# Fewer calls for the expert dot products inside the top-k heads, more of them in the later stages

## The chip, the cores and the metric

The kernel runs on one core of one Trainium2 chip. The metric is the device time of one execution in microseconds; lower is better. In the profile, PE is TensorE, DVE is VectorE, ACT is ScalarE, POOL is GpSimd and SP is SyncE.

## The reference

Two layers on 512 tokens of width 1024. Each layer is a mixer (attention with a convolution in layer 0, gated linear attention in layer 1) and a PEER block, which retrieves single-neuron experts. The change touches the PEER block alone; RMS norms and the mixers are left out here:

```python
def block(xb):                                   # 128 tokens
    q = (xb @ w_query).reshape(t, PEER_HEADS, 2, PEER_HALF)          # 8 heads
    scores = jnp.einsum('thpd,hpnd->thpn', q, sk)                    # 2 x 128 keys
    s_val, s_idx = lax.top_k(scores, PEER_TOPK)                      # 16
    cand = s_val[:, :, 0, :, None] + s_val[:, :, 1, None, :]
    c_val, c_idx = lax.top_k(cand.reshape(t, PEER_HEADS, 256), PEER_TOPK)
    ...
    expert = i1 * N_KEYS + i2                                        # of 16384
    gate = jax.nn.softmax(c_val, axis=-1)
    act = jax.nn.gelu(jnp.einsum('thkd,td->thk', expert_u[expert], xb))
    return jnp.einsum('thk,thkd->td', gate * act, expert_v[expert])
```

Each token has 8 heads times 16 picks, 128 experts.

## The kernel before, in words

The 512 tokens are split into four tiles of 128. **Three of them (384 tokens) take the dense way**: TensorE computes the activations of all 16384 experts and the sum over all of them, with gates that are zero where an expert is not picked. **The first tile takes the gathered way**: for each of its 128 picks GpSimd fetches one row of `u` per token, and later one row of `v` per token, by an indirect DMA (L452), 128 rows of 4 KB (524,288 bytes) at once, into a ring of five buffers (`NBUF`). VectorE consumes them. `dots` (L965, its instruction is L969) multiplies a fetched row by the normalised input and sums it up to one column of `hg`; `sums` (L974, its instruction is L978) adds a fetched row of `v`, times its coefficient, to the residual `x[:, 0]`. Each frees its buffer for the next fetch (`gat_free`). A layer has 128 dots and then 128 sums. Between them ScalarE applies the gelu to `hg` and VectorE multiplies by the gates.

Every matrix of experts is read in float32 and split into two bf16 halves: ScalarE writes the high half (`split_hi`, L630) and VectorE the low half (`split_lo`, L941, called as `ahead(n)` for tile n). TensorE waits for both before each tile (L1479 to L1481, 24 matmuls) and before each quarter of a value group (L1547).

The PEER block of a layer goes through these stages, in the same order on all engines:

- **Heads**, h = 0 to 7. TensorE does eight tiles per head; behind the first it computes the queries of the head (L1490, evicted by ScalarE at L665), behind the second the scores (L1497, L671). VectorE does the top-k of the head for all four token tiles (L991 to L1057), a chain of small instructions with drains between them. It ends with the index of the experts of the first token tile (`eidx`, L1062), which releases 16 more fetches. Between the steps of the chain stand `ahead(RING * h + 4)` to `ahead(RING * h + 11)` and, by hand, calls of `dots`. In head h only rows of earlier heads are there to be taken, so head 0 has none.
- **Tail of the heads**, tiles 64 to 71. TensorE transposes the picks (L1509), ScalarE exponentiates (L708), VectorE makes the gates (L1072 to L1076), TensorE transposes them (L1514).
- **Batches**, tiles 72 to 119. For each tile VectorE builds one-hot matrices (L1096 to L1100), TensorE multiplies them (L1526, L1527), and so a dense matrix of gates for the 384 tokens is made. It goes to DRAM, as do the activations. Tiles 120 to 127 follow without batches.
- **Values**, groups k = 0 to 31 of 72 matmuls each. For each group SyncE loads 2 MB of `v`, the activations (768 KB) and the gates (640 KB). VectorE multiplies them (`scale(k)`, L1111 to L1116), ScalarE rounds the product (`high(k)`, L693), VectorE makes the rest (`low(k)`, L1120), and TensorE waits for that before the group (`clo_ready`). VectorE then does the four low halves of group k + 1.

The last dot must come before the gelu of `hg`, which stands in group `HG_GROUP`; sums begin there. The last sum must come before the residual of token tile 0 is closed, after group 31.

Of the kernel before, what the change touches and what calls it, by code (L numbers as in the profile page):

```python
# [15 lines left out]
P = 128  # L16
# [17 lines left out]
PH = 8  # L34
# [14 lines left out]
NBUF = 5  # L49
NST = NCK - 2  # L50
B0 = NK // 2 + 8
HG_GROUP = 3
CAND = 128


# [30 lines left out]
def build(nc, x_d, cols_d, const_d, hot_d, relb_d, wmix_d, wz_d, wg2_d, wq_d, u_d, ur0_d, ur1_d, v0_d, v1_d,  # L86
# [7 lines left out]
    with ExitStack() as ctx:  # L94
# [369 lines left out]
        def _(act):  # L464
# [167 lines left out]
            def peer(L):  # L632
                T0, G0 = STREAM * L, 2 * NG * L
                def ahead(n):
                    if n < TPG:
                        act.wait_ge(first_in[n], 16 * (L + 1))
                    split_hi(T0 + n, n % RING, arrival(L, n) if n >= TPG and n % TPG == 0 else None)
# [74 lines left out]
                for k in range(NG):  # L712
                    if k:
                        high(k)
                    if k + 1 < NG:
                        for q in range(TPG):
                            ahead(NK + TPG * (k + 1) + q)
                    if k == HG_GROUP:
                        act.wait_ge(hg_ready, L + 1)
# [11 lines left out]
        def _(dve):  # L731
# [211 lines left out]
            def peer(L):  # L943
                T0, G0 = STREAM * L, 2 * NG * L
                def ahead(n):
                    if n < TPG:
                        dve.wait_ge(first_in[n], 16 * (L + 1))
                    split_lo(T0 + n, n % RING, arrival(L, n) if n >= TPG and n % TPG == 0 else None)
# [8 lines left out]
                taken = [0]  # L957

                def taken_in():
                    n = 2 * P * L + taken[0]  # L960
                    taken[0] += 1
                    dve.wait_ge(gat_in[n % NBUF], 16 * (n // NBUF + 1))
                    return ring[n % NBUF], (n % P)

                def dots(count):  # L965
                    for _ in range(count):
                        if taken[0] < P:
                            row, g = taken_in()
                            dve.tensor_tensor_reduce(row, row, xg, 1.0, 0.0, ALU.mult, ALU.add,  # L969
                                                     hg[:, g:g + 1]).then_inc(gat_free, 1)  # L970
                            if taken[0] == P:
                                dve.drain().then_inc(hg_ready, 1)

                def sums(count):  # L974
                    for _ in range(count):
                        if taken[0] < 2 * P:
                            row, g = taken_in()
                            dve.scalar_tensor_tensor(x[:, 0], row, cf[:, g:g + 1], x[:, 0], ALU.mult, ALU.add).then_inc(gat_free, 1)  # L978
                            dve.drain()

                for h in range(PH):
# [1 line left out]
                    ahead(RING * h + 4)  # L983
                    ahead(RING * h + 5)

                    late = 0 < h < PH - 1
                    dots(3 if h else 0)
                    dve.wait_ge(s_out, h + (PH * L + 1))
                    ahead(RING * h + 6)
                    for tt, s in pairs:  # L990
# [2 lines left out]
                    for tt, s in pairs:  # L993
                        dve.max_index(idx[:, tt, s, 0:8].bitcast(U32), val[:, tt, s, 0:8], sc[:, tt, s])
                        dve.match_replace(sc2[:, tt, s], val[:, tt, s, 0:8], sc[:, tt, s], -3e38)
                    dots(1 if h else 0)
                    dve.drain()
                    for tt, s in pairs:
                        dve.max(val[:, tt, s, 8:16], sc2[:, tt, s])
# [1 line left out]
                    ahead(RING * h + 7)  # L1001
                    for tt, s in pairs:
                        dve.max_index(idx[:, tt, s, 8:16].bitcast(U32), val[:, tt, s, 8:16], sc2[:, tt, s])
                    dots(2 if h else 0)
                    dve.memset(cand[:, :, 64:80], -3e38)
                    for first, rows, width in ((0, 4, TOPK), (4, TOPK - 4, 4)):
                        a = val[:, :, 0, first:first + rows].unsqueeze(3).to_broadcast([P, TT, rows, width])
# [5 lines left out]
                    for tt in range(TT):  # L1013
                        dve.max(cval[:, tt, 0:8], cand[:, tt])
                    ahead(RING * h + 8)
                    dots(1 if h else 0)
                    dve.drain()
                    for tt in range(TT):
                        dve.max_index(cidx[:, tt, 0:8].bitcast(U32), cval[:, tt, 0:8], cand[:, tt])
# [2 lines left out]
                    for tt in range(TT):  # L1022
                        dve.max(cval[:, tt, 8:16], cand2[:, tt])
                    ahead(RING * h + 9)
                    dots(1 if h else 0)
                    dve.drain()
                    for tt in range(TT):
                        dve.max_index(cidx[:, tt, 8:16].bitcast(U32), cval[:, tt, 8:16], cand2[:, tt])
# [10 lines left out]
                    dve.tensor_tensor(side, ci, shift, ALU.logical_shift_right)  # L1039
                    dve.tensor_tensor(rank[1].bitcast(U32), ci, low, ALU.bitwise_and)  # L1040
                    ahead(RING * h + 10)
                    dots(1 if late else 0)
                    dve.drain()
                    dve.tensor_scalar(rank[0].bitcast(U32), side, TOPK - 1, None, ALU.bitwise_and)
                    dve.drain()
                    for s in range(2):
# [7 lines left out]
                        if s == 0:  # L1054
# [6 lines left out]
                    at = slice(h * TOPK, (h + 1) * TOPK)  # L1061
                    dve.scalar_tensor_tensor(eidx[:, at], picks[:, 0, 0, at], float(NK), picks[:, 1, 0, at],  # L1062
                                             ALU.mult, ALU.add).then_inc(eidx_ready, 1)
                    dots(3 if late else 0)

                dve.drain()
                pv = picks[:, 2].rearrange("p a (h k) -> p (a h) k", h=PH)
# [24 lines left out]
                def hots(b):  # L1092
                    hot = [oh[:, k, b % 2].rearrange("p (a n c) -> p a n c", n=P, c=2) for k in range(3)]
                    every = iota_2[:].unsqueeze(1).to_broadcast([P, BT // 2, P, 2])
                    dve.wait_ge(g_built, NB * L + b + 1)
                    dve.tensor_tensor(hot[1], every, along(1, b), ALU.is_equal)  # L1096
                    dve.tensor_tensor(hot[0], every, along(0, b), ALU.is_equal)
                    dve.drain()
                    dve.tensor_tensor(hot[2], hot[1], along(3, b), ALU.mult)
                    dve.tensor_tensor(hot[1], hot[1], along(2, b), ALU.mult).then_inc(oh_ready, 1)  # L1100

                def scale(k):


                    s, g = k % 2, (k + NG - 2) % NG
                    if k < 2:
                        dve.wait_ge(gelu_done, NK * L + TPG * (g + 1) + 2)
                    dve.wait_ge(gh_in[s], (32 * (NG // 2) - 16) * L + 16 + 32 * (k // 2))
                    h4 = hst[s].rearrange("p q (c t) -> p q c t", t=CHK)
                    early = h4[:, :, 0:NST]  # L1110
                    dve.tensor_tensor(early, early, gr[s].rearrange("p c q t -> p q c t"), ALU.mult)  # L1111
                    dve.wait_ge(g_read, NB * (L + 1) + 2)
                    for c in range(2):
                        late = h4[:, :, NST + c]
                        dve.tensor_tensor(late, late, gst[c][:, g].rearrange("p (q t) -> p q t", q=TPG), ALU.mult)
                    dve.drain().then_inc(cf_ready, 1)  # L1116

                def low(k):
                    dve.wait_ge(chi_ready, NG * L + k + 1)
                    dve.tensor_tensor(clo[k % 2], hst[k % 2], chi[k % 2], ALU.subtract).then_inc(clo_ready, 1)  # L1120

                for n in range(NK // 2 + 3, NK):
                    if B0 <= n < B0 + NB:
                        hots(n - B0)
                    ahead(n + TPG)
                    if n == NK - 4:
                        scale(0)
                    if n == NK - 2:
                        low(0)
                    if B0 <= n < B0 + NB:  # L1130
                        dots(n % 2)
                    elif B0 <= n < NK - 2:
                        dots(2)
                for q in range(TPG):
# [4 lines left out]
                for k in range(NG):  # L1139
                    if k > 1:  # L1140
                        scale(k)
                        if k > HG_GROUP:
                            sums(1)
                        else:
                            dots(1)
                        low(k)
                    if 0 < k < NG - 1:
                        for q in range(TPG):
                            ahead(NK + TPG * (k + 1) + q)
                    if k < HG_GROUP:  # L1150
                        dots(4 if k else 2)
                    else:
                        if k == HG_GROUP:
                            assert taken[0] == P
                            dve.wait_ge(hg_act, L + 1)
                            dve.tensor_tensor(cf, hg, gt[:, 0], ALU.mult)
                            dve.drain()
                        sums(4)
                assert taken[0] == 2 * P
                dve.drain().then_inc(x_new, 1)  # L1160
                for tt in range(GT, TT):
# [22 lines left out]

            mixer0()
            peer(0)
            mixer1()
            peer(1)


# [470 lines left out]
```

## Time and profile before

| | |
|---|---|
| time, median of 3 runs | 2967.38 us (2964.68 to 2969.16) |
| the profiled execution | 2967.38 us, its span 2965.6 us |
| TensorE busy | 2882.7 us, 97% of the span |
| VectorE busy | 2318.7 us, 78% |
| ScalarE busy | 1010.6 us, 34% |
| GpSimd busy | 731.3 us, 25% |
| chain that ended last | TensorE 68%, VectorE 19% |
| DMA | 775.21 MB, mean 261 GB/s |

The difference of 1.8 us between an execution and its span lies outside the instructions. In layer 0 the head stage runs from about 276 to 662 us, its tail to 700, the batches to 932, and the value stage from 966 to 1460. Layer 1 has the same stages from about 1772 us on.

### The profile page before, as it was taken

To read this page: it belongs to the slowest core of one execution; us is meant where nothing else is said; L and a number is where in the kernel's file an instruction comes from. 1 tells how busy PE (TensorE), PEld (TensorE's weight loads), DVE (VectorE), ACT (ScalarE), POOL (GpSimd) and SP (SyncE) were. 2 spreads that over 40 slices of the span, in tenths; PEclk is the share of its full clock that TensorE was granted. 3 is DMA by queue.
4 is the path that set the end of the run, shared out by engine and by line. 5 is a ranking of instruction groups with operands and counts; after the bars stand their busy time and mean duration, and the time that the engine had idled before them with its cause. 6 is when DMAs were issued, how large, how long until landed. Compare 5 with 4: busy or idle time off the path is not lost.

```text
span 2965.6 us, 39736 instructions
## 1 busy us (share of the span) xinstructions
PE 2882.7 (97%) x14563; PEld 1527.8 (52%) x14632; DVE 2318.7 (78%) x4251; ACT 1010.6 (34%) x1335; POOL 731.3 (25%) x518
## 2 busy tenths in 40 slices
PE   8998999999999999999999889999999999999998
PEld 4454555556666444444444445555556664444443
DVE  5853799998888899999400336999988888999995
ACT  2162323224554333333321122232245544333333
POOL 0000133330112445544000001232301124445540
PEclk9999999999999999999999999999999999999999
DMA  4202577776998999999211124777769989999993
GB/s 151 85 29 108 212 261 291 259 263 223 320 310 311 388 404 394 397 395 390 73 63 70 57 94 181 260 283 257 259 237 308 308 317 399 391 396 400 394 400 116
DMA packets 210407, 775.21 MB, mean 261 GB/s; under 512 B 15445, under 2 KB 97497, under 8 KB 190218
## 3 DMA queue, kind: packets, MB, share of 16 engines
q1 hardware_dynamic: 45698, 416.58, 36.9%
q0 software_dynamic: 73728, 268.47, 24.4%
q10 hardware_dynamic: 90888, 89.14, 8.6%
q8 instruction: 32, 0.52, 0.1%
q14 instruction: 61, 0.50, 0.0%
HBM read 681.59 MB, written 92.54 MB: 261 GB/s over the span
## 4 chain that ended last, share of the span: by engine, by line
PE 68%; DVE 19%; issue 4%; DMA 3%; DVEq 3%; PEld 1%; ACT 1%; PEldq 0%; ACTq 0%; POOL 0%; SPq 0%
PE ps L1547 28%; PE ps L1479 6%; PE ps L1481 6%; PE ps L1480 6%; PE ps L1231 5%; PE ps L1240 5%; DVE arena L969 5%; PE ps L1260 3%; DVE arena L941 3%; DMA arena<-in_ur,arena 3%; PE ps L1490 2%; PE ps L1527 1%; PE ps L1526 1%; PEld ps L1547 1%; DVE arena L1053 1%
## 5 line engine op out<-in xcount | busy, mean ns | idle before, releaser
L1547 PE MATMUL ps<-arena 128*128 128x512 bf16 x4541 | 992.2, 379 | 5.3 <-DVE arena L1120 1.5
L452 POOL DMA_INDIRECT arena<-in_ur,arena x256 | 331.2, 1294 | 1679.8 <-DVE arena L969 948.3
L1547 PEld LDWEIGHTS ps<-arena 128*128 128x128 bf16 x4608 | 450.5, 98 | 546.4 <-issue 2.9
L941 DVE TENSOR_TENSOR arena<-arena 128x1024 bf16<-128x1024 f32 x512 | 611.5, 1220 | 130.4 <-ACT arena L630 88.4
L1479 PE MATMUL ps<-xnh,arena 128*128 128x384 bf16 x2048 | 673.1, 329 | 32.6 <-DVE xnl L767 13.3
L1481 PE MATMUL ps<-xnh,arena 128*128 128x384 bf16 x2048 | 673.4, 329 | 0.0
L1480 PE MATMUL ps<-xnl,arena 128*128 128x384 bf16 x2048 | 673.2, 329 | 0.0
L630 ACT ACTIVATE arena<-arena 128x1024 bf16<-128x1024 f32 x512 | 525.5, 1049 | 186.8 <-PE ps L1547 104.3
L452 POOL DMA_INDIRECT arena<-in_v,arena x256 | 399.1, 1559 | 406.2 <-DVE x_res L978 339.5
L978 DVE SCALAR_TENSOR_TENSOR x_res<-arena,x_res 128x1024 f32<-128x1024 f32 x256 | 328.6, 1283 | 20.8 <-issue 0.4
L969 DVE CUSTOM_DVE_ANT_0 arena<-arena 128x1024 f32<-128x1024 f32 x256 | 306.3, 1219 | 34.2 <-DMA arena<-in_ur,arena 33.5
L657 ACT ACTIVATE arena<-ps 128x384 f32<-128x384 f32 x256 | 125.6, 491 | 531.7 <-PE ps L1481 520.4
L1479 PEld LDWEIGHTS ps<-xnh,arena 128*128 128x128 bf16 x2048 | 201.5, 98 | 168.6 <-issue 45.7
L1481 PEld LDWEIGHTS ps<-xnh,arena 128*128 128x128 bf16 x2048 | 201.6, 98 | 135.7 <-issue 4.8
L1480 PEld LDWEIGHTS ps<-xnl,arena 128*128 128x128 bf16 x2048 | 201.6, 98 | 131.5 <-issue 10.3
L693 ACT ACTIVATE arena<-arena 128x1536 bf16<-128x1536 f32 x64 | 94.9, 1483 | 507.6 <-DVEq L1116 507.6
L1490 PE MATMUL ps<-xnT,arena 128*128 128x512 f32 x512 | 222.3, 592 | 0.0
L1490 PEld LDWEIGHTS ps<-xnT,arena 128*128 128x128 f32 x512 | 96.8, 190 | 115.8 <-issue 114.8
L1231 PE MATMUL ps<-xnT,arena 128*128 128x512 f32 (+1 forms) x336 | 148.5, 605 | 2.5 <-ACT xnT L487 2.5
L1240 PE MATMUL ps<-arena,xnT 128*128 128x512 f32 x320 | 139.1, 598 | 0.0
L1120 DVE TENSOR_TENSOR arena<-arena 128x1536 bf16<-128x1536 f32 x64 | 112.5, 1758 | 21.8 <-ACT arena L693 21.8
L504 ACT ACTIVATE arena<-ps 128x512 f32<-128x512 f32 (+1 forms) x49 | 29.1, 597 | 266.3 <-PE ps L1231 130.3
(188 smaller groups left out, 2322.9 us busy)
## 6 DMA issues: line engine op xcount, KB each, us to landing
arena<-in_v SPq DMA_DIRECT2D x64, 2048.0 KB
arena<-in_u SPq DMA_DIRECT2D x62, 2048.0 KB
h_scratch<-arena ACTq DMA_DIRECT2D x60, 768.0 KB
arena<-h_scratch SPq DMA_DIRECT2D x60, 768.0 KB
arena<-gate_scratch SPq DMA_DIRECT2D x64, 640.0 KB
arena<-in_wmix SPq DMA_DIRECT2D x15, 2048.0 KB, 7.9
gate_scratch<-xnT ACTq DMA_DIRECT2D x10, 2048.0 KB
gate_scratch<-arena ACTq DMA_DIRECT2D x10, 2048.0 KB
```

The source lines that it names most:

```text
L452: pool.indirect_dma_start(ring[n % NBUF], None, ur_d[L] if g < P else vr_d[L], at).then_inc(gat_in[n % NBUF], 16)
L630: act.activation(hi[:, s], raw[s // TPG][:, s % TPG], ACT.Copy).then_inc(hi_ready, 1)
L941: dve.tensor_tensor(lo[:, s], raw[s // TPG][:, s % TPG], hi[:, s], ALU.subtract).then_inc(lo_ready, 1)
L969: dve.tensor_tensor_reduce(row, row, xg, 1.0, 0.0, ALU.mult, ALU.add, hg[:, g:g + 1]).then_inc(gat_free, 1)
L978: dve.scalar_tensor_tensor(x[:, 0], row, cf[:, g:g + 1], x[:, 0], ALU.mult, ALU.add).then_inc(gat_free, 1)
L1231: last = pe.matmul(bank[0:cols_of], wblk[b % 2][:, kd, at], xnT[:, kd], start=kd == 0, stop=kd == KD - 1)
L1240: last = pe.matmul(bank, xnT[:, kd, at], wblk[b % 2][:, kd], start=kd == 0, stop=kd == KD - 1)
L1479: pe.matmul(ps[:, j % 2, 0:TD], uh, xnh[:, kd], start=kd == 0, stop=False)
L1480: pe.matmul(ps[:, j % 2, 0:TD], uh, xnl[:, kd], start=False, stop=False)
L1481: last = pe.matmul(ps[:, j % 2, 0:TD], ul, xnh[:, kd], start=False, stop=kd == KD - 1)
L1490: last = pe.matmul(ps[:, 2 + s], wq[:, kd, at], xnT[:, kd], start=kd == 0, stop=kd == KD - 1)
L1547: last = pe.matmul(ps[:, 2 + 2 * tt + dh], c, v[:, TPG * s + q, dh * 512:(dh + 1) * 512], start=False, stop=stop and c is cl)
```

## The change

Two numbers for the calls of `dots` replace hand-placed ones. In a head, the calls between the steps of the top-k chain go; four rows are taken before the wait for the scores, and in heads 1 to 6 five more behind the index. In the batch stage two of three tiles have a dot instead of every second. In the value stage group 0 has four dots at its end instead of two, and the gelu of `hg`, with the first sums, moves from group 3 to group 6.

```diff
+HEAD_DOTS = 9
+V_DOTS = 5
-HG_GROUP = 3
+HG_GROUP = 6
...
-                    late = 0 < h < PH - 1
-                    dots(3 if h else 0)
+                    if h:
+                        dots(HEAD_DOTS // 2)
                     dve.wait_ge(s_out, h + (PH * L + 1))
...
-                    dots(1 if h else 0)
...
-                    dots(2 if h else 0)
+
...
-                    dots(1 if h else 0)
...
-                    dots(1 if h else 0)
...
-                    dots(1 if late else 0)
...
                     dve.scalar_tensor_tensor(eidx[:, at], picks[:, 0, 0, at], float(NK), picks[:, 1, 0, at],
                                              ALU.mult, ALU.add).then_inc(eidx_ready, 1)
-                    dots(3 if late else 0)
+                    if 0 < h < PH - 1:
+                        dots(HEAD_DOTS - HEAD_DOTS // 2)
...
                     if B0 <= n < B0 + NB:
-                        dots(n % 2)
+                        dots(1 if n % 3 else 0)
                     elif B0 <= n < NK - 2:
                         dots(2)
...
                     if k < HG_GROUP:
-                        dots(4 if k else 2)
+                        dots(V_DOTS - 1)
                     else:
                         if k == HG_GROUP:
-                            assert taken[0] == P
                             dve.wait_ge(hg_act, L + 1)
                             dve.tensor_tensor(cf, hg, gt[:, 0], ALU.mult)
                             dve.drain()
-                        sums(4)
+                        sums(V_DOTS - 1)
```

A call of `dots` takes no row once all 128 are taken.

## Rows read from the trace of the kernel before

**Rows 1.** Busy time in stages: batches, start of values, the rest (layer 0)

```profile
core 0: us, PE busy (x) PEld busy (x) DVE busy (x) ACT busy (x) POOL busy (x), PEclk, DMA share, GB/s
...
700.00:932.00 232.00, 232.00 (x1920) 156.84 (x1919) 205.16 (x288) 119.44 (x144) 26.35 (x23) 1.00 0.88 298
...
966.00:998.00 32.00, 31.13 (x143) 14.03 (x146) 26.86 (x34) 12.93 (x13) 13.93 (x9) 1.00 0.98 402
998.00:1405.00 407.00, 405.63 (x1860) 184.54 (x1887) 382.93 (x347) 140.42 (x132) 196.58 (x128) 1.00 1.00 396
```

**Rows 2.** Waits of TensorE, heads and tail, layer 0, then layer 1

```profile
PE ps L1479 <- issue: 9.7, 6, 3.0
...
PE ps L1479 <- DVE arena L941: 6.4, 3, 3.0
PE ps L1479 <- issue: 3.2, 3, 1.4
PE ps L1509 <- DVE arena L1057: 0.9, 1, 0.9
```

**Rows 3.** Timelines of VectorE and TensorE (start, duration, what, [idle before])

```profile
513.87 1.21 DVE L941 TENSOR_TENSOR arena<-arena 128x1024 bf16<-128x1024 f32 x1
...
515.17 0.32 PE L1479 MATMUL ps<-xnh,arena 128*128 128x384 bf16 x1 [2.99 <-issue]
```

**Rows 4.** Busy time in the first and last of six stretches

```profile
516.30:519.70 3.40, 3.40 (x13) 1.65 (x11) 3.32 (x21) 1.06 (x1) 0.94 (x1) 0.50 0.96 357
...
2178.60:2182.00 3.40, 3.00 (x10) 1.46 (x11) 1.95 (x5) 2.50 (x3) 0.00 (x0) 0.50 0.01 5
```

**Rows 5.** Query evictions, heads 0 to 4; indices, heads 1 to 3; index, head 0

```profile
L665 ACT ACTIVATE arena<-ps x5: 1024/1024/1025, 296.2 to 483.0; 128x1024 f32<-128x1024 f32 x5
...
L1062 DVE SCALAR_TENSOR_TENSOR arena<-arena x3: 175/175/176, 388.5 to 484.8; 128x16 uint32<-128x16 f32 x3
...
335.24 0.18 DVE L1062 SCALAR_TENSOR_TENSOR arena<-arena 128x16 uint32<-128x16 f32 x1
```

**Rows 6.** Timelines of VectorE and TensorE, start of the values, layer 0

```profile
976.47 1.22 DVE L969 CUSTOM_DVE_ANT_0 arena<-arena 128x1024 f32<-128x1024 f32 x1
...
977.62 1.22 DVE L969 CUSTOM_DVE_ANT_0 arena<-arena 128x1024 f32<-128x1024 f32 x1
...
994.75 1.22 DVE L969 CUSTOM_DVE_ANT_0 arena<-arena 128x1024 f32<-128x1024 f32 x1 [2.76 <-DMA arena<-in_ur,arena]
...
998.00 5.34 PE L1547 MATMUL ps<-arena 128*128 128x512 bf16 x24 [0.77 <-DVE arena L1120]
```

**Rows 7.** Timeline of GpSimd in head 6; list of DMA issues

```profile
636.09 1.68 POOL L452 DMA_INDIRECT arena<-in_ur,arena  x1 [9.53 <-DVE arena L969]
...
642.63 0.94 POOL L452 DMA_INDIRECT arena<-in_ur,arena  x1 [0.30 <-issue]
...
arena<-in_u SPq DMA_DIRECT2D x8, 512.0 KB, 5.5
```

**Rows 8.** Timelines of the three engines in the tail, layer 0

```profile
681.82 0.87 PE L1509 MATMUL ps<-const,arena 128*128 128x128 f32 x6 [0.93 <-DVE arena L1057]
...
684.59 0.63 ACT L708 ACTIVATE arena<-arena 128x512 f32<-128x512 f32 x1
...
687.04 2.35 DVE L941 TENSOR_TENSOR arena<-arena 128x1024 bf16<-128x1024 f32 x2
```

**Rows 9.** Groups of instructions of the value stage (busy, mean ns, idle before)

```profile
L978 DVE SCALAR_TENSOR_TENSOR x_res<-arena,x_res 128x1024 f32<-128x1024 f32 x256 | 328.6, 1283 | 20.8 <-issue 0.4
...
L1120 DVE TENSOR_TENSOR arena<-arena 128x1536 bf16<-128x1536 f32 x64 | 112.5, 1758 | 21.8 <-ACT arena L693 21.8
L1111 DVE TENSOR_TENSOR arena<-arena 128x1280 f32<-128x1280 f32 x64 | 95.4, 1491 | 5.4 <-issue 0.4
L693 ACT ACTIVATE arena<-arena 128x1536 bf16<-128x1536 f32 x64 | 94.9, 1483 | 507.6 <-DVEq L1116 507.6
```

**Rows 10.** Timeline of VectorE, start of the values, layer 1

```profile
2487.20 1.23 DVE L969 CUSTOM_DVE_ANT_0 arena<-arena 128x1024 f32<-128x1024 f32 x1 [1.73 <-DMA arena<-in_ur,arena]
```

**Rows 11.** Timeline of VectorE, end of the values, layer 0

```profile
1454.05 1.22 DVE L1164 TENSOR_TENSOR x_res<-x_res,ps 128x1024 f32<-128x1024 f32 x1 [13.28 <-PEq L1571]
```

## The prediction

> **What bounds the kernel now.** I read the busy time by stage first. TensorE works without a break in the batch stage (232.0 of 232 us) and for 405.6 of 407 us of the value stage, and VectorE is never its equal there, 205.2 and 382.9 us [rows 1]. So the kernel is bound by TensorE, and another engine costs time only where TensorE stands. The list of waits gives those places [rows 2]: in the head stage and the four tiles behind it, layer 0 has six waits of 9.7 us in all and one of 0.9 us before the transposes of the picks; layer 1 has 6.4, 3.2 and again 0.9 us. Together that is 21.1 us. Some of these waits carry no releaser, but the two timelines side by side name it: VectorE ends the low half of tile 40 (`ahead(RING * h + 8)` of head 4) at 513.87 + 1.21 = 515.08, and TensorE, idle for 2.99 us, starts that tile at 515.17 [rows 3]. Layer 1 names L941 outright.
>
> Each larger stall also costs clock. Six stretches of 3.4 us, each beginning a microsecond or so after the engine resumed work, or at it, ran with a granted clock of 0.50, the 1.2 GHz level; the first and the last stand in [rows 4]. At half speed 3.4 us do 1.7 us of work, so the six lose 10.2 us. In all 21.1 + 10.2 = 31.3 us hang on VectorE being late in the head stages. That is the most that lighter heads can give back.
>
> **Why VectorE is late.** TensorE's own period per head is (483.0 - 296.2) / 4 = 46.7 us, by the evictions of the queries; VectorE's, from index to index over heads 1 to 3, is (484.8 - 388.5) / 2 = 48.15 us [rows 5]. It falls 1.45 us behind per head, uses up its lead by head 4, and from then on TensorE pays: stalls before heads 5 and 7, and at the end of the stage, where tiles follow each other without the queries between them.
>
> **The change part by part.** Two dots in a row are 1.15 us apart (976.47 and 977.62) [rows 6]. Counting calls:
>
> - Heads 1 to 6 hold 3+1+2+1+1+1+3 = 12 dots each now, head 7 holds 8. They will hold 4+5 = 9, and 4. Per layer 80 become 58.
> - Batch stage: 24 become 32. The six tiles behind it keep 12, and one stays at the start of the value stage. So 103 instead of 117 are taken when group 0 begins.
> - Value stage: group 0 has 4 instead of 2, groups 1 and 2 have the same 4 and 5, and the dots then run on into group 5. Sums start in group 6 instead of 3 and end in group 31 instead of 28, five per group as before.
>
> *Heads.* 3 x 1.15 = 3.4 us less makes VectorE's period 48.15 - 3.4 = 44.7 us, 2.0 us under TensorE's. Head 0 has no dots, and its index comes at 335.24, 7.7 us before the next eviction of queries (296.2 + 46.7 = 342.9) [rows 5], that is some 10 us after the first tile of the next head began. From the scores on, a head will run as head 0 does, so this place repeats. The critical low half (`+ 8`) stands the same steps ahead of the index as now, less three dots, and so comes several microseconds before its tile (I reckon 6). The stalls before heads 5 and 7 go: 2.99 + 0.33 + 3.00 us and two slow stretches in layer 0, 6.4 us and two in layer 1, so 19.5 us.
>
> *The burst.* Five dots behind the index, two low halves and four dots make nine rows nearly in a row, with five buffers. Four rows must be fetched meanwhile. GpSimd needs 0.94 us for a fetch when VectorE is elsewhere and 1.68 when it runs dots [rows 7], so with the gaps between them issues lie some 2 us apart, the fourth at about 8 us. A 512 KB load lands 5.5 us after its issue where DMA is not crowded [rows 7], so the ninth row comes some 13 us after the burst began; the dots are done at 14 to 14.5 us instead of 12.7 (five dots, two low halves, four dots). VectorE has 2.0 us to spare there, because it would otherwise wait for the scores. I cost this at nothing. With 3 us of waiting per burst the period would be 47.7 and the lead used up again by the last head (a rival below).
>
> *End of the heads.* The index of head 7 comes some 10 us earlier, so the waits before tiles 65 and 66, the transposes and tile 68 go: 4.3 and 4.1 us, and one slow stretch each. What is late next is the gate chain. The transposes end at 681.82 + 0.87 = 682.69, the exponential behind a table load at 684.59 + 0.63, the gates at about 687.1, and the low half of tile 69 1.15 us later, 688.2 [rows 8]: 5.5 us after the transposes. TensorE will fill that with one tile at full clock and three transposes, 4.4 us. It keeps about 1.3 us per layer with the wake-ups. The tails give 6.05 - 1.3 and 5.8 - 1.3, together 9.2 us.
>
> So the head side gives 19.5 + 9.2 = 28.7 us.
>
> *Batch stage.* Eight more dots are 9.2 us, and VectorE stood 26.8 of 232 us there [rows 1]. Two tiles with a dot and one without average less than a tile of TensorE, and a row has more than a tile's time to arrive. Cost: nothing; bound: the 9.2 us if that cover were gone.
>
> *Start of the value stage.* Here DMA moves 402 GB/s with its engines 98% busy [rows 1], and refills are late already. In layer 0 the row that goes into the buffer of the dot of 977.62 (five rows on) is the one that VectorE waits for until 994.75, 17 us later. `low(2)` hangs on it, and TensorE waits 0.77 us for `low(2)` at 998.00 [rows 6]. With two more dots in group 0 the two rows that group 1 now takes from full buffers are gone, so that late row becomes the third of group 1's four instead of the single one behind `scale(2)`. The two next rows, 524 KB each at 402 GB/s, land 1.3 us apart, at 996.0 and 997.3. The working: fourth dot until 997.2; `scale(2)` 1.49 and twice 0.28 with its drain, 2.0 us, 999.2; ScalarE's `high(2)` 1.48, 1000.9; `low(2)` 1.76, 1002.6 [rows 9]. TensorE starts group 2 at 1002.8 instead of 998.0: 4.9 us. In layer 1 the same row comes at 2487.20, so that `low(2)` ended 1.16 + 1.76 later, at 2490.1 [rows 9, 10]; by the steps above it will end at 2495.0, and of the 4.9 us I take 1.0 as margin, since TensorE did not wait there: 3.9 us. Waits of 3 us cost a slow stretch [rows 3, 4], so 1.7 us each on top. Sum: 8.8 + 3.4 = 12.2 us. Lower bound 0 (the refills come when wanted); upper bound some 9 us more per layer, if each extra refill comes as late after its forerunner as this one did. I take the middle, worked from the rows of this very place.
>
> A rule speaks against this cost. The Trainium skill (DMA: Bandwidth & Descriptors, "Anatomy of one DMA — SWDGE (gpsimd) path") puts a DMA issued from GpSimd at 2.0 us plus bytes over 436 GB/s. By that estimate a row takes 3.2 us, no refill would be late and the time would be that of the first rival. The 17 us in the trace do not agree.
>
> *The rest of the value stage.* Per group the load stays. At its end three sums (1.28 us each [rows 9]) come behind `low(31)`, where VectorE now stands 13.28 us [rows 11]. Nothing.
>
> **The sum.** 28.7 - 12.2 = 16.5 us less. The profiled execution took 2967.38 us with a span of 2965.6, and is itself the median of the three runs: 2967.4 - 16.5 = 2950.9, say 2951 (-0.56%).
>
> **The rivals.**
>
> 1. The refills are not late at the value stage's start, for instance because the next 2 MB load also starts later. Then 2967.4 - 28.7 = 2939. Against it stands DMA at 98%. Chance 0.18.
> 2. The burst of nine starves. At 3 us lost per burst the period is 47.7, 1.0 over TensorE's; the lead lasts through the heads, but the tail's 9.2 us are not won: 2967.4 - 19.5 + 12.2 = 2960. At 3.4 us the period is today's, 48.15, nothing of the 28.7 is sure, and the kernel is slower by up to the 12.2. For it: fetches that take nearly twice as long beside dots [rows 7]. Against it: DMA is not crowded at that place, and half the burst finds its rows in the buffers. Chance 0.15. In the Trainium skill (Trainium Architecture — The Big Picture, "What this means for kernel authors") the port pair of VectorE and GpSimd is an exclusive lock rather than a split of bandwidth. Were GpSimd shut out for the whole burst, this rival would be the outcome; a fetch of 1.68 us during dots shows a delay and not a stop.
> 3. Slower: the debt is never repaid. Five rows and the loads of v, h and gates are about 6.2 MB per group of 15.4 us, 400 GB/s, and DMA already gives 396 at a share of 1.00 [rows 1]. If two early rows push the h and gate loads late in every later group, `scale(k)` and TensorE with it slip each time. It decides from 28.7 / 58 = 0.5 us per group; at 1 us the time is 2967 - 29 + 58 = 2996. Against it: the same rate runs today with TensorE idle for 1.4 of 407 us, and a wait of 5 us at group 2 lets DMA move 2 MB. Chance 0.08.
>
> **How the numbers follow.** My forecast has 0.52, with a range of its own of 2945 to 2956; 0.07 stays for what I don't see. The range of 2938 to 2964 takes in rival 1 and the milder end of rival 2, and leaves out the third. A measurement here tells 0.2%, 6 us, from no change: faster is my case, rival 1 and half of rival 2, 0.78; same is a third of rival 2 and most of the unseen, 0.12; slower is rival 3 and the worst of rival 2, 0.10.
>
> **What would show it.** After: no TensorE wait of 3 us in the head stage and no slow clock there; VectorE's idle time there now waits for ScalarE's scores; index to index 46.7 us from head 1 on; about 1.3 us of idle between the gate transposes and tile 69. At group 2 of each layer a wait of 4 to 6 us for `low` (L1120 now), behind dots that wait for DMA. Wrong would be: waits of that kind in every group, waits for fetched rows of over 3 us in each head, or none at group 2.

## The result and the profile after

| | before | after |
|---|---|---|
| median, side by side on one chip | 2968.27 us (2964.68 to 2969.21) | 2992.11 us (2980.25 to 2996.37) |
| the profiled execution, its span | 2967.38 us, 2965.6 us | 2995.14 us, 2993.3 us |

The change makes the kernel slower by 0.7%: ratio 1.0073, 95% interval 1.0045 to 1.0100. The forecast was 2951.0, its range ended at 2964. The spread has grown too: 16 us between executions instead of 5 (8 us in the 19 executions of the kernel before that stand beside the last experiments).

I cut both traces at the evictions of the dense tiles (L657 before, L659 now: tiles 0, 63, 71, 119, 127) and at the first and last matmul of the values. The differences are those of the two profiled executions.

| stage | layer 0, before to after | layer 1 | change | forecast |
|---|---|---|---|---|
| heads | 378.9 to 380.3 | 378.8 to 377.4 | 0.0 | -19.5 |
| tail | 38.9 to 37.1 | 38.6 to 35.8 | -4.6 | -9.2 |
| batches | 230.3 to 238.4 | 230.4 to 238.9 | +16.6 | 0 |
| values | 499.8 to 506.8 | 497.9 to 507.0 | +16.1 | +12.2 |
| all else | | | -0.3 | 0 |
| span | | | +27.8 | -16.5 |

Busy time by stage in the kernel after, layer 0, answers to [rows 1] (columns as there):

```profile
core 0: us, PE busy (x) PEld busy (x) DVE busy (x) ACT busy (x) POOL busy (x), PEclk, DMA share, GB/s
288.00:662.00 374.00, 366.17 (x1879) 208.28 (x1877) 313.37 (x1037) 106.12 (x140) 92.09 (x63) 0.99 0.62 223
...
700.00:940.00 240.00, 233.25 (x1926) 156.05 (x1924) 210.84 (x302) 118.78 (x145) 36.51 (x32) 1.00 0.89 304
972.00:1012.00 40.00, 34.61 (x150) 15.13 (x151) 32.35 (x41) 13.02 (x13) 18.03 (x10) 0.92 0.96 385
1012.00:1425.00 413.00, 411.58 (x1887) 187.15 (x1912) 381.18 (x359) 141.30 (x132) 201.80 (x130) 1.00 0.99 391
```

The batch stage, where TensorE had not stood at all, now has 6.75 us in which it does. TensorE's waits in heads and tail, then in the batches, of each layer (us in total, times, longest) answer to [rows 2]:

```profile
PE ps L1477 <- issue: 8.3, 6, 3.0
PE ps L1477 <- ACT arena L632: 1.6, 1, 1.6
PE ps L1507 <- DVE arena L1055: 0.7, 1, 0.7
...
PE ps L1477 <- DVE arena L943: 5.4, 2, 2.7
PE ps L1477 <- issue: 1.8, 2, 1.4
...
PE ps L1524 <- DVE arena L1099: 6.7, 6, 1.9
...
PE ps L1524 <- DVE arena L1099: 7.4, 6, 2.1
```

The stalls in the heads have moved and not gone, and six waits per layer for the one-hots (L1099) have come. The third new place is group 2 of the values. VectorE and TensorE there, layer 0, then the same wait in layer 1; this answers to [rows 6]:

```profile
990.34 1.22 DVE L971 CUSTOM_DVE_ANT_0 arena<-arena 128x1024 f32<-128x1024 f32 x1
992.82 1.23 DVE L971 CUSTOM_DVE_ANT_0 arena<-arena 128x1024 f32<-128x1024 f32 x1 [1.25 <-DMA arena<-in_ur,arena]
995.42 1.23 DVE L971 CUSTOM_DVE_ANT_0 arena<-arena 128x1024 f32<-128x1024 f32 x1 [1.37 <-DMA arena<-in_ur,arena]
1000.99 1.22 DVE L971 CUSTOM_DVE_ANT_0 arena<-arena 128x1024 f32<-128x1024 f32 x1 [4.33 <-DMA arena<-in_ur,arena]
...
1005.61 1.76 DVE L1119 TENSOR_TENSOR arena<-arena 128x1536 bf16<-128x1536 f32 x1 [0.19 <-ACT arena L695]
...
1007.61 2.72 PE L1545 MATMUL ps<-arena 128*128 128x512 bf16 x6 [5.29 <-ACT arena L632]
...
2516.88 3.57 PE L1545 MATMUL ps<-arena 128*128 128x512 bf16 x8 [6.69 <-ACT arena L632]
```

The releaser printed is not the last one: `low(2)` ends at 1005.61 + 1.76 = 1007.37, and TensorE starts at 1007.61.

### The profile page after: what moved, and what is told of

The parts are those of the page before. It is cut to its first block, busy times and chain, and to the rows that moved or that the text cites. A ratio compares the mean times of both kernels' runs of the same rounds, so it can differ in the third digit from the quotient of the medians.

```text
span 2993.3 us, 39736 instructions
## 1 busy us (share of the span) xinstructions
PE 2889.2 (97%) x14563; PEld 1528.3 (51%) x14632; DVE 2320.4 (78%) x4251; ACT 1008.0 (34%) x1335; POOL 763.3 (25%) x518
## 4 chain that ended last, share of the span: by engine, by line
PE 49%; DVE 16%; issue 12%; PEld 8%; DMA 5%; DVEq 4%; ACT 2%; POOL 2%; ACTq 1%; PEldq 1%; SPq 0%
PE ps L1545 13%; PEld ps L1545 8%; PE ps L1477 5%; PE ps L1478 5%; PE ps L1479 5%; PE ps L1229 5%; PE ps L1238 5%; DMA arena<-in_ur,arena 4%; DVE arena L943 4%; PE ps L1258 3%; POOL arena L454 2%; PE ps L1488 2%; PE ps L1524 1%; PE ps L1525 1%; DVE arena L1051 1%
## 5 line engine op out<-in xcount | busy, mean ns | idle before, releaser
L454 POOL DMA_INDIRECT arena<-in_ur,arena x256 | 364.4, 1423 | 1758.7 <-DVE arena L971 1004.1
L1545 PEld LDWEIGHTS ps<-arena 128*128 128x128 bf16 x4608 | 451.6, 98 | 560.4 <-ACT arena L632 12.9
L632 ACT ACTIVATE arena<-arena 128x1024 bf16<-128x1024 f32 x512 | 525.0, 1048 | 192.3 <-PE ps L1545 107.4
L659 ACT ACTIVATE arena<-ps 128x384 f32<-128x384 f32 x256 | 125.4, 490 | 532.6 <-PE ps L1479 532.4
```

The lines of the kernel that those rows point to most:

```text
L454: pool.indirect_dma_start(ring[n % NBUF], None, ur_d[L] if g < P else vr_d[L], at).then_inc(gat_in[n % NBUF], 16)
L632: act.activation(hi[:, s], raw[s // TPG][:, s % TPG], ACT.Copy).then_inc(hi_ready, 1)
L1545: last = pe.matmul(ps[:, 2 + 2 * tt + dh], c, v[:, TPG * s + q, dh * 512:(dh + 1) * 512], start=False, stop=stop and c is cl)
```

## The two mechanisms that I had not seen

**Batches.** A stretch of the three engines in the kernel after (start, duration, what, [idle before]): ScalarE issues the gate store, 8.6 us later the store of the activations (`h_store`, L663), and everything behind that issue shifts:

```profile
739.02 0.39 ACTq L687 DMA_DIRECT2D gate_scratch<-arena  x1
...
747.60 2.96 ACTq L663 DMA_DIRECT2D h_scratch<-arena  x1
...
750.60 1.06 ACT L632 ACTIVATE arena<-arena 128x1024 bf16<-128x1024 f32 x1 [1.99 <-issue]
...
751.69 1.23 DVE L943 TENSOR_TENSOR arena<-arena 128x1024 bf16<-128x1024 f32 x1 [2.38 <-ACT arena L632]
...
752.84 1.22 DVE L971 CUSTOM_DVE_ANT_0 arena<-arena 128x1024 f32<-128x1024 f32 x1
...
756.69 0.23 PE L1524 MATMUL ps<-arena 128*128 128x128 bf16 x1 [0.41 <-DVE arena L1099]
```

The issue holds ScalarE for 2.96 us, its high half (L632) comes late, VectorE's low half behind it, then the dot, then the one-hots. Nine of the twelve stores of this stage in layer 0 are issued like that, in 2.96 to 4.39 us. VectorE was busy for 210.84 us there and waited 24.2 us for the high half:

```profile
DVE arena L943 <- ACT arena L632: 24.2, 17, 3.1
```

That is 235.0 of 240 us. Cut at tiles 71 and 119, nothing is left over: 210.6 us busy, 24.2 in this wait and 3.6 in gaps of at most 0.15 us make the 238.4 of the stage. So VectorE's chain was the bound. In the kernel before, the same wait in 700 to 932 us had already been

```profile
DVE arena L941 <- ACT arena L630: 25.4, 35, 2.7
```

and with 205.16 us of work that left 1.4 of 232 us free [rows 1], where I had counted 26.8 as room. The eight dots came on top of a wait that did not shrink to make room for them.

**Heads.** The burst behind the index of head 5, layer 0. Its nine dots are those of 580.08 to 584.66 (five) and of 588.08, 589.95, 597.14 and 598.42:

```profile
579.99 0.17 DVE L1060 SCALAR_TENSOR_TENSOR arena<-arena 128x16 uint32<-128x16 f32 x1
...
581.57 1.68 POOL L454 DMA_INDIRECT arena<-in_ur,arena  x1 [31.42 <-DVE arena L971]
...
583.56 1.99 POOL L454 DMA_INDIRECT arena<-in_ur,arena  x1 [0.30 <-issue]
...
585.59 0.34 ACTq L663 DMA_DIRECT2D h_scratch<-arena  x1
...
585.85 1.99 POOL L454 DMA_INDIRECT arena<-in_ur,arena  x1 [0.30 <-issue]
...
587.50 0.33 SPq L375 DMA_DIRECT2D arena<-in_wq  x1
...
589.95 1.23 DVE L971 CUSTOM_DVE_ANT_0 arena<-arena 128x1024 f32<-128x1024 f32 x1 [0.65 <-DMA arena<-in_ur,arena]
597.14 1.23 DVE L971 CUSTOM_DVE_ANT_0 arena<-arena 128x1024 f32<-128x1024 f32 x1 [5.96 <-DMA arena<-in_ur,arena]
...
608.49 1.23 DVE L943 TENSOR_TENSOR arena<-arena 128x1024 bf16<-128x1024 f32 x1
...
609.82 0.48 PE L1477 MATMUL ps<-xnh,arena 128*128 128x384 bf16 x1 [2.99 <-issue]
```

The second refill is there 6.4 us after its issue (583.56 to 589.95), the third only after 11.3 (585.85 to 597.14): the store of the activations (768 KB) was issued just before it, the next head's query weights (1152 KB) just behind it. The burst waits for 6.6 us where 2.0 were to spare, and from 606.83 TensorE stands for 2.99 us, for the low half that ends at 608.49 + 1.23. The store is issued 17.6 us after the eviction of tile 8h + 8 in heads 1 to 6, whatever VectorE does. The index comes 5.7, 6.7, 9.3 and 12.8 us after that eviction in heads 1 to 4. So each late burst puts more of the next one's refills behind the store: the lateness feeds itself, which fits the spread of the times. From index to index over heads 1 to 3 it is (476.9 - 379.8) / 2 = 48.5 us, where I had reckoned 44.7. Over the whole stage a fetch of a row takes 7.3 us in the median from issue to landing (4.9 to 11.5).

## The experiments

Medians; each ratio is to the kernel before on the same chip. The layers' stage lengths are cut as above.

**The batch pattern alone**, in the kernel before:

```diff
-                        dots(n % 2)
+                        dots(1 if n % 3 else 0)
```

> The kernel before with the batch stage alone changed (a dot in two of three tiles). Theory A (the batch stage's growth comes from where the dots stand: ScalarE is blocked for 3 to 4 us every fourth tile by its store of activations, and a dot in the tile behind that makes the one-hots late): TensorE waits for L1100 in about six tiles of each layer, batch stage 238 us instead of 230 in each, and with the earlier end of the dots about 2967 + 16 - 1 = 2982 us. Rival A' (it comes from the changed head stage or from fetches, not from this pattern): batch stage 230 us, time 2967.

2981.24 against 2963.93 us, ratio 1.0055 (1.0038 to 1.0072). Batches 240.1 and 238.4 us. TensorE's waits there, layer 0:

```profile
PE ps L1526 <- DVE arena L1100: 8.3, 6, 2.0
```

The eight dots cost about 17 us by themselves. As expected.

**Two more dots in value group 0 alone**, in the kernel before (groups 1 and 2 had four already):

```diff
-                        dots(4 if k else 2)
+                        dots(4)
```

> The kernel before with value group 0 alone changed (four dots for two). Theory B (refills late behind the two extra dots): TensorE waits 5 to 7 us before group 2 of each layer, followed by some 7 us at half clock, 3.4 us lost: 2967 + 18 = 2985 us. Rival B' (that wait is due to what happened earlier, since 103 and not 117 dots were taken by then): no wait above 1 us, 2967.

2982.14 against 2963.93 us, 1.0064 (1.0047 to 1.0081). The wait before group 2 is there without the rest of the change, 7.30 us in layer 0 and 7.56 in layer 1; the values take 508.8 and 508.0 us:

```profile
1000.44 4.00 PE L1547 MATMUL ps<-arena 128*128 128x512 bf16 x9 [7.30 <-ACT arena L630]
```

**Where the dots of the batches stand**, in the kernel after; 36 dots instead of 32, none where `n % 4` is 2:

```diff
-                        dots(1 if n % 3 else 0)
+                        dots(1 if n % 4 != 2 else 0)
```

> The changed kernel with a dot in every tile of the batch stage but those with n mod 4 = 2 (36 instead of 32 dots). Theory A (position): batch stage back to about 230 us in each layer although it has more dots, 2992 - 16 = 2976. Rival A'' (number: VectorE has too little time for more than 24): batch stage 238 us or more, 2992 or above.

2986.52 against 2963.93 us, 1.0087 (1.0066 to 1.0109). Batches 239.0 and 239.1 us:

```profile
PE ps L1524 <- DVE arena L1099: 6.2, 9, 1.0
```

Nine short waits in place of six longer ones, and nearly the same sum. My theory that the position alone was at fault fell: the stage did not come back to 230 us. The rival holds for the stage, though not for the time (2992 or above), and number alone does not carry it either: eight dots more cost 8 us, and these four, otherwise placed, only 0.2 to 0.6 more. How place and number share the loss stays open.

**Group 0 back to two dots**, in the kernel after:

```diff
-                        dots(V_DOTS - 1)
+                        dots(V_DOTS - 1 if k else 2)
```

> The changed kernel with two dots in value group 0 instead of four. Theory B: the waits of 5.3 and 6.7 us before group 2 shrink to about 1 us and the half clock behind them goes: 2992 - 17 = 2975. Rival B': the waits stay, 2992.

2971.61 against 2963.93 us, 1.0024 (1.0010 to 1.0039). No wait at group 2; the values take 498.9 and 498.0 us. Heads were 368.5 us in layer 0 and 382.8 in layer 1 of one execution: the instability in one trace.

**The same 58 dots per layer, but between the steps of the heads**, in the kernel after (the last added line stands at three places):

```diff
-                    if h:
-                        dots(HEAD_DOTS // 2)
+                    late = 0 < h < PH - 1
+                    dots(3 if h else 0)
...
+                    dots(1 if h else 0)
...
+                    dots(2 if late else 0)
...
+                    dots(1 if late else 0)
...
-                    if 0 < h < PH - 1:
-                        dots(HEAD_DOTS - HEAD_DOTS // 2)
```

> The changed kernel with the same 58 dots of the heads put back between the steps of the top-k chain (3+1+2+1+1+1 in heads 1 to 6, 3+1 in head 7). Theory C (the burst of nine starves on its refills once it meets the load of the next head's weights, and so the gain of lighter heads is lost): no TensorE wait of 3 us and no half clock in either head stage, heads 368 us per layer instead of 380 and 377, 2992 - 20 = 2972 us. Rival C' (VectorE's lateness there has another cause than the burst): stalls stay, 2992.

2971.39 against 2966.35 us, 1.0016 (1.0006 to 1.0025). Heads 368.5 us in both layers, with no wait of TensorE, and the store of the activations where it was: fewer dots do give the gain, the burst takes it back. VectorE waits for fetched rows for 4.8 us in each head stage (34.7 and 32.0 in the kernel after), and the index keeps its place, 12.5 to 12.9 us behind the tile in heads 1 to 6.

**The store of the activations two tiles earlier**, in the kernel after. It is then issued ahead of the gate store and not 8.6 us behind it:

```diff
+                    if n % TPG == TPG - 1 and n // TPG < NG - 2:
+                        h_store(n // TPG)
                     if B0 <= n < B0 + NB:
                         gates_out(n - B0)
-                    if n >= TPG and n % TPG == 1 and n // TPG - 1 < NG - 2:
-                        h_store(n // TPG - 1)
```

> The changed kernel with ScalarE's store of activations issued two tiles earlier, ahead of the store of gates instead of 9 us behind it. Theory A2 (the store stands in a queue still full of the gate store's packets and blocks ScalarE for 3 to 4 us, and the wait for the high half behind it takes the time that the eight extra dots need): L663 takes 0.3 us everywhere, no wait for L1099, batch stage 230 us instead of 238, 2992 - 16 = 2976. Rival A3 (VectorE's own work per tile is too long with 32 dots, whatever ScalarE does): L663 short, waits stay, 2992.

2951.91 against 2966.35 us, 0.9954 (0.9937 to 0.9971). Durations of the store's issue (minimum, median, maximum in ns) in the batches of layer 0, first in the kernel after, then here:

```profile
L663 ACTq DMA_DIRECT2D h_scratch<-arena x12: 338/3292/4392, 709.1 to 929.2; - x12
```

```profile
L663 ACTq DMA_DIRECT2D h_scratch<-arena x12: 338/338/352, 704.8 to 916.8; - x12
```

Batches are 230.3 us again with all 32 dots, and VectorE's wait for the high half, cut at tiles 71 and 119, falls from 24.2 to 15.2 us. That was expected; that the heads fell to 368.5 us as well, with TensorE busy throughout, was not:

```profile
283.00:666.00 383.00, 383.00 (x1983) 219.03 (x1983) 332.43 (x1085) 114.48 (x151) 91.97 (x63) 1.00 0.64 230
```

In head 5 of layer 0 the third refill is issued at 576.15 and the fourth at 578.44. Their dots wait little:

```profile
581.95 1.25 DVE L971 CUSTOM_DVE_ANT_0 arena<-arena 128x1024 f32<-128x1024 f32 x1 [1.20 <-DMA arena<-in_ur,arena]
...
584.72 1.22 DVE L971 CUSTOM_DVE_ANT_0 arena<-arena 128x1024 f32<-128x1024 f32 x1 [1.51 <-DMA arena<-in_ur,arena]
```

The third row takes 5.8 us instead of 11.3. These rows do not part two effects, since this burst also starts 3.8 us earlier behind its tile. And the burst is not cured: VectorE still waits 20.0 us for rows in the first head stage, and the index slips from 5.7 to 10.0 us behind the tile between heads 1 and 7. The stage ends before the lead is used up.

**The same earlier store in the kernel before.**

> The kernel before with the same earlier store. TensorE has no wait in its batch stage, so by theory A2 the time stays within 2 us of 2964; only L661 falls from 1.9 to 3.6 us to 0.3. By rival A3 the same, so this run tells only whether the earlier store costs anything by itself.

2950.84 against 2966.35 us, 0.9948 (0.9931 to 0.9964): a miss. Heads 371.7 us in both layers, batches unchanged at 230.3. TensorE's waits between tiles 0 and 63 of layer 0 were 6.3 us with two of 3.0, followed by two stretches at half clock. They are now 2.7 us, the longest 1.2, and no slow clock follows. The rows go on to 668 us and so take in some of the tail:

```profile
PE ps L1479 <- issue: 4.5, 5, 1.2
PE ps L1479 <- ACT arena L630: 1.4, 1, 1.4
```

VectorE's waits for fetched rows fall from 10.3 to 4.5 us. The kernel before paid for the same collision at its three trailing dots, and I had put all of it down to VectorE's work. That work is still too long by itself: the indices of heads 1 to 3 stand where they stood, 48.1 us apart, and 3.2 of the 10.4 us stay.

**Which place the store hurts.** The earlier store in the head stage alone, then from tile 67 on alone, in the kernel after:

```diff
+                    if n % TPG == TPG - 1 and n < NK // 2:
+                        h_store(n // TPG)
...
-                    if n >= TPG and n % TPG == 1 and n // TPG - 1 < NG - 2:
+                    if n > NK // 2 + 1 and n % TPG == 1 and n // TPG - 1 < NG - 2:
```

> The changed kernel with the store of the activations issued two tiles earlier (at the fourth tile of its own group) in the head stage alone; from tile 69 on it is issued where it was. Theory A (the store of 2 MB, issued as the burst behind the index begins, is what delays the burst's refills): the head stages are as with the earlier store everywhere, 368.5 us each and without a TensorE wait behind a late low half, and the batch stage keeps its 238.4 us with the six waits for the one-hots. Time about 2972: 2951.9 + 2 x 8.2 + some 3. Theory B (what helped the heads was something that the batch stage or the gate store handed on from the layer before): the head stages stay at 377 to 380 us with stalls behind low halves of 1.5 to 3 us, and the time is 2990.

> The changed kernel with the store of the activations issued two tiles earlier from tile 67 on alone; in the head stage it is issued where it was. Theory A (each place has its own cost): the batch stage is 230.3 us, the issue of the store takes 0.34 us there and no wait for one-hots is left, while the head stages keep 377 to 380 us and their stalls. Time about 2975: 2992 - 2 x 8.3. Theory B (one cause for both): the head stages are cured too, 368.5 us each, and the time is 2952.

Heads alone: 2969.87 against 2963.59 us, 1.0022 (1.0012 to 1.0033); heads 368.5 and 368.5, batches 238.5 and 238.9. Batches alone: 2973.23 (2960.81 to 2975.44), 1.0021 (1.0009 to 1.0033); batches 230.3 and 230.3, heads 375.9 and 368.5. Each place has its own cost. The store is one of 768 KB, not of the 2 MB that my expectation says. The second trace is of one of the two fastest executions (2960.83 us), and shows a layer that happened to escape the head stalls. VectorE's waits for fetched rows in the first head stage, heads alone:

```profile
DVE arena L973 <- DMA arena<-in_ur,arena: 17.1, 17, 3.4
```

**The query weights almost gone**, in the kernel after. Heads 1 to 7 load 64 columns of their block and compute with what head 0 left in the rest, so the output is wrong; the kernel leaves out this load and no work of an engine:

```diff
-                    sp.dma_start(qk_w, wq_d[L, h]).then_inc(wq_in, 16)
+                    if full:
+                        sp.dma_start(qk_w, wq_d[L, h]).then_inc(wq_in, 16)
+                    else:
+                        sp.dma_start(qk_w[:, 0:64], wq_d[L, h][:, 0:64]).then_inc(wq_in, 16)
```

> The changed kernel in which every head but the first of a layer loads only 64 columns of its block of query weights and keys, so that those heads compute with the columns of the first one: the load that runs into the burst behind the index is almost gone from DMA, the store of the activations is not. Theory A (the store alone is enough to make the burst's refills late): DMA-caused waits of VectorE in the first head stage stay near 35 us and the head stages at 377 to 380 us. Theory B (it takes the sum of store, weights and refills): the DMA-caused waits fall to under 15 us and the head stages to about 369 us, so some 18 to 20 us less in all, 2972.

2972.56 us in one execution, beside 2963.59 for the kernel before. Heads 368.5 and 369.2 us with the store where it was. The same wait, in the kernel after and here:

```profile
DVE arena L971 <- DMA arena<-in_ur,arena: 34.7, 17, 6.0
```

```profile
DVE arena L974 <- DMA arena<-in_ur,arena: 16.6, 15, 3.1
```

A fetch takes 6.5 us in the median from issue to landing instead of 7.3, and 9.4 at most instead of 11.5. That speaks for a share of the weights, but does not show it. The 16.6 us, and 22.9 in layer 1, miss the 15 that I had set; in layer 1 the index still slips to 12.8 us by head 7. And of the eight head stages that I have with store and weights in place (the kernel after, the two runs on its batch dots and group 0, and the early store in the batches alone), two also took 368.5 us without a stall, with 21.5 and 20.9 us of such waits. What is shown is the store's share: with it moved, all four head stages traced took 368.5 us.

**All three mended**: the kernel after with the dots spread in the heads, the earlier store, and two dots in group 0.

> The changed kernel with all three mended: dots of the heads spread, earlier store, two dots in value group 0. If theories A2, B and C hold together, nothing of the losses remains and the head stage gives back its 28 us: 2964 - 27 = 2937 us. If a loss moves on instead (lighter stages shift transfers into each other), between 2945 and 2975.

2937.53 (2935.35 to 2939.35) against 2966.35 us, 0.9901 (0.9885 to 0.9918). It beats both kernels. TensorE's waits from the first tile to the last value matmul of layer 0:

```profile
PE ps L1514 <- DVE arena L1077: 1.2, 1, 1.2
PE ps L1479 <- issue: 0.6, 1, 0.6
PE ps L1547 <- DVE arena L1121: 0.3, 1, 0.3
```

## Why the prediction was wrong

- **Heads, -19.5.** The count of dots was right and its cover failed. With the same 58 dots spread over the chain the heads take 368.5 us in both layers, 10.4 and 10.3 less than before: 20.7. The kernel after realises none of it. The reading of why VectorE is late was right only in part: the store alone, moved in the kernel before, gives 7.2 of the 10.4.
- **The burst, costed at nothing.** This is the first step that failed. I took the 5.5 us landing of a plain 512 KB load "where DMA is not crowded" and said that it isn't at that place; a fetch of a row in the head stage took 7.3 in the median. I had not listed what else is issued there: the store of the activations and the query weights, both inside the burst. The third refill took 11.3 us, and rival 2, with its chance of 0.15, came true in this step, in its worse half: the debt per burst exceeds what the lighter heads give (index to index 48.5 us and not 44.7), and of the 28.7 only 4.6 arrive. By the Trainium skill (DMA: Bandwidth & Descriptors, "Anatomy of one DMA — SWDGE (gpsimd) path") a row would have taken 3.2 us, by my estimate; the trace does not agree, its shortest fetch took 4.3. As the prediction said, VectorE's dots only delay GpSimd's work on a fetch (1.68 to 1.99 us) and don't stop it; the fourth was issued 8.1 us behind the start of the burst, as reckoned, and what came late was the data.
- **End of the heads, -9.2.** Where VectorE keeps its lead the tail takes 34.4 us (early store), 4.5 and 4.2 less, 8.7 in all. In the kernel after the lead is used up, and 4.6 are left.
- **Batch stage, costed at nothing.** The second step that failed, and the dearer one: +8.1 and +8.5 us, near the bound of 9.2 per layer that I had set aside. The sum over the stage hid that VectorE's 26.8 idle us were nearly all waits for ScalarE's high half (25.4), and that part of ScalarE's delay was a store whose issue already took 2.1 us in the median there (L661). With more dots that median is 3.3 us. Why it grew is not settled; that the place behind the gate store makes it long is what the run with the earlier store shows. The growth is not what costs the time: in layer 1 of the kernel before the median was 3.1 us already (2.38 to 3.54 behind a gate store), and TensorE did not stand. The loss takes the held-up ScalarE and the eight dots together; without either, the stage takes 230.3 us.
- **Start of the values, +12.2.** Mechanism, place and chain as forecast; two terms too small. The idle time is 5.29 + 6.69 - 0.77 = 11.2 instead of 8.8, since the group's last row came 4.3 us late and not 1.3, and since I took off 1.0 in layer 1 that was not there. By the stage lengths 16.1 - 11.2 = 4.9 go to the clock, where I had 3.4. The 17 us of the late row ran from the dot that freed its buffer; its fetch was issued at 979.95, so that 14.8 us are the fetch's own, still far from 3.2.
- **The rest of the values, nothing.** Right: there is no wait of TensorE from group 3 to the end, and rival 3, the one case that ended slower by as much, is refuted although its time of 2996 is near.

The sum that the runs give: -4.6 + 16.6 + 16.1 - 0.3 = 27.8. By medians, the kernel after stands 23.8 us above the kernel before. Against the kernel before on its own chip, undoing group 0 leaves 7.7 of it, spreading the heads 5.0, and the early store -14.4. Of the 38.2 us of the early store, its two halves give 17.5 (23.8 - 6.3) and 14.2 (23.8 - 9.6), 6.5 short of the whole. The trace with the early store in the heads alone shows most of it: its wait before group 2 of layer 0 is 9.39 us instead of 5.29, and the values take 511.3 us there, 4.5 more than in the kernel after. Why that wait grew I leave open.

## What to carry to other kernels

Idle time of a helper engine is not room as it stands: look what it waited for, and add that wait to its work before putting more into the stage. Before bunching the consumers of a ring, list every DMA issued within the burst, on all queues; a landing time from a quiet stretch doesn't hold there. And the place of a store in an engine's program is worth a look by itself: moving it by two tiles was worth 15 us in the kernel as it stood.

## What the hardware did that I had not expected

- The same issue of a 768 KB store takes ScalarE 0.34 us, or 2.96 to 4.39 us when it follows 8.6 us behind a 2 MB store to the gates' scratch in its queue (1.79 to 4.65 in layer 1, and 1.84 to 3.54 in the kernel before). Issued just ahead of that store, 17.8 us behind the one before, it takes 0.34 again. The distance is not all of it: one such issue, at 728.33, took 0.60.
- The clock falls while TensorE still waits. Busy time around group 2, layer 0, in the kernel after:

```profile
1006.00:1006.80 0.80, 0.00 (x0) 0.00 (x0) 0.80 (x1) 0.80 (x2) 0.80 (x1) 0.50 0.93 364
...
1011.10:1011.90 0.80, 0.80 (x4) 0.24 (x3) 0.80 (x2) 0.00 (x0) 0.00 (x0) 0.50 1.01 374
...
1012.80:1013.60 0.80, 0.80 (x6) 0.38 (x4) 0.80 (x3) 0.00 (x0) 0.28 (x1) 1.00 1.02 430
```

The granted clock is 0.50, the 1.2 GHz level, at 1006.0, before the engine resumes at 1007.61, and 1.00 by 1012.8; in a finer cut it is still 0.51 in 1012.4 to 1012.6 and 1.00 behind that. Work from 1007.6 to about 1012.6 ran at half speed, 5.0 us, of which half is lost: 2.5 us for this wait instead of the 1.7 that I took from shorter ones. The stage agrees: it grew by 7.0 us in layer 0, of which 5.29 - 0.77 = 4.5 are idle time.
